# State space tiles: squares added in pairs on GpSimd, their products with ones behind the intra product

## The chip, the cores and the metric

The kernel runs on one core of one Trainium2 chip. The metric is the device time of one launch in microseconds. The kernel before took 3885.12 us (median of 3 runs, 3883.11 to 3887.59).

## The reference

One inference step of a two-layer streaming encoder for a prompt of 1024 frames and 8 samples of 16 frames, 1152 columns in all, width 1024, in float32. The even layer runs RWKV-7 and Mamba-2 as parallel mixers behind one input and one output projection; the odd layer runs HGRN2. Each layer ends in a SwiGLU network. The part that matters here is the Mamba-2 mixer (16 heads of 64, two groups with a state of 128):

```python
cb = jnp.einsum('bclgn,bcsgn->bclsg', cc, bc)
y_intra = jnp.einsum('bclsg,bclsgh,bcsghp->bclghp', cb, decay_ls, xd)
...
y_inter = jnp.einsum('bclgn,bcghpn,bclgh->bclghp', cc, s_in, jnp.exp(acum))
...
y = y + d_skip[:, None] * xs
y = y.reshape(*y.shape[:2], W_B) * jax.nn.silu(z.astype(jnp.float32))
return group_rms_norm(y, norm_w, G_B), conv_new, s_new
```

`group_rms_norm` divides each of the two groups of 512 channels of a frame by the root of its mean square and weighs it by `norm_w`.

## The kernel before

The stage `mamba_tiles` works on nine tiles of 128 columns: eight of the prompt (t = 0 to 7) and one with all samples (t = 8, LAST). Channels lie on the partitions in eight blocks of 128, the columns of the tile beside each other. Each engine has its own order, written out by hand as a loop over t from -1; in one round the tile t is in its middle part, u = t + 1 in its front part and t - 1 in its last part. Semaphores join the engines.

TensorE, one round: `inter(t)` (L3252, the state product), `square_sum(t - 1)` (L3364), `intra(t)` (L3270, sixteen heads), `turn_x(u)` (L3279, the transposes of the next x), `grams(u)`, half of a transpose of a sample's state (L3324), `turn_y(t)` (L3307), `state(t)` (L3314), the other half, and four `segments(u, i)` (L3301).

VectorE, one round: `inter(t)` (L3113, takes the state product out of PSUM), `finish(t - 1)` (L3129, eight instructions that weigh the tile by root and weight, into `g.act`), `intra(t)` (L3122, adds the intra product), `weigh(u)` (L3138, takes the turned x), `mask_CB(u)` (L3147), `skip(t)` (L3165, eight instructions), `scale_state(t)` (L3151) and `add_state(t)` (L3158), `gate(t)` (L3172), `to_end(u)` (L3178), `scores(u)` (L3184, two instructions that multiply the decays of eight heads each by the masked score).

ScalarE, one round: `spread_decays(u, 0)` (L3020, eight instructions), `root(t - 1)` (L3044 and L3047), `spread_decays(u, 1)`, copies and exponentials (L3051, L3033, L3027), and `square(t)` (L3038), which writes the squares of the gated tile t, 128x1024, into `squares(t)`: a part of `g.act` that belongs to a later tile, for the last tile `zt`.

GpSimd sets a small mask and, when the x of the last tile is there, copies four small pieces (L3099). SP loads x and z: the x of tile u + 1 (L2997) and the z of tile u (L2999) go out when the gate of tile u - 1 is done.

The sum over the channels of a group is a product of `ones` with each of its four blocks of squares, accumulated in PSUM. Waits that touch the change: the intra products wait for `att_done` (the scores) and `xd_done`; VectorE's `intra` waits for them; `weigh` waits for `turn_x`; `skip` waits for `out_done` (the finish before); `square_sum(t)` waits for the squares and for the exponentials of the tile after; `segments` and the transposes of the last state wait for `var_ln`, the first half of the root.

Of the kernel before, what the change touches and what calls it, by code (L numbers as in the profile page):

```python
# [18 lines left out]
ALU = mybir.AluOpType  # L19
# [9 lines left out]
NT = T // P  # L29
# [2922 lines left out]
def mamba_tiles(nc, g, A, S, S_samples, decays, shared, xbc, first_x, states_in, ssm_out, following):  # L2952
# [4 lines left out]
    with Phase(nc, "mamba") as ph:  # L2957
# [11 lines left out]
        squares = lambda t: g.act[:, PAIRS:KACT, (t + 1) * P:(t + 2) * P] if t < NT - 1 else zt[:, :, :]  # L2969
# [1 line left out]
        bank = ph.ps("bank", [P, 8, BANK])  # L2971
        (x_in0, x_in1, z_in, mask_set, RL_done, xT, xd_done, CB_mm, CB_done, B_out, seg_mm, seg_out, att_done, xde_done,
         inter_mm, intra_mm, y1_done, y2_done, st_mm, S_scaled, S_done, yT, skip_done, yz_done, sq_done, ss_mm, var_ln,
         rs_done, out_done, Ce_done, xde_split, seq_scaled, seq_T, seq_in, last_T, last_out) = ph.sems(
            "x_in0 x_in1 z_in mask_set RL_done xT xd_done CB_mm CB_done B_out seg_mm seg_out att_done xde_done "
            "inter_mm intra_mm y1_done y2_done st_mm S_scaled S_done yT skip_done yz_done sq_done ss_mm var_ln "
            "rs_done out_done Ce_done xde_split seq_scaled seq_T seq_in last_T last_out")
        stored = ph.sems("out0 out1 out2")
        x_in = (x_in0, x_in1)
        block = ph.block()  # L2980
        LAST = NT - 1
# [29 lines left out]
        @block.scalar  # L3011
        def _(act):
            nc.scalar.preload_act_table_set("natural_log_exp_and_others")

            def spread_decays(u, half):
                if u:
                    act.wait_ge(seg_mm, 4 * u)
                mask = g.notafter if u == LAST else g.notafter128
                for h in range(half * GH, half * GH + GH):
                    ins = nc.scalar.activation(RL[:, h, :], mask[:, :], ACT.Identity, scale=decays.tok[:, 1, u, h:h + 1])  # L3020
                ins.then_inc(RL_done, 1)

            def take_B(u):
                act.wait_ge(CB_done, u + 1)
                if u >= 2:
                    act.wait_ge(st_mm, u - 1)
                nc.scalar.copy(B_tok[:, u % 2, :, :].rearrange("p g n -> p (g n)"), bank[:, 2, 256:512]).then_inc(B_out, 1)  # L3027

            def take_seg(u, i):
                act.wait_ge(seg_mm, 4 * u + i + 1)  # L3030
                if u:
                    act.wait_ge(intra_mm, u)
                nc.scalar.activation(att[:, i * QH:(i + 1) * QH, :].rearrange("p h l -> p (h l)"), bank[:, i % 2, :],  # L3033
                                     ACT.Exp, scale=-1.0).then_inc(seg_out, 1)

            def square(t):
                act.wait_ge(yz_done, t + 1)
                nc.scalar.activation(squares(t), y[:, :, :], ACT.Square).then_inc(sq_done, 1)  # L3038

            def root(t):  # L3040
                act.wait_ge(ss_mm, t + 1)
                if t:
                    act.wait_ge(out_done, t)
                nc.scalar.activation(rs[:, :, :].rearrange("p g c -> p (g c)"), bank[:, sums_at(t), 0:256], ACT.Ln,  # L3044
                                     bias=g.eps[:, 1:2], scale=1.0 / (WB // 2)).then_inc(var_ln, 1)
                act.wait_ge(var_ln, t + 1)
                nc.scalar.activation(rs[:, :, :], rs[:, :, :], ACT.Exp, scale=-0.5).then_inc(rs_done, 1)  # L3047

            def take_sequence(b, i):
                act.wait_ge(seq_T, 2 * b + i + 1)  # L3050
                nc.scalar.copy(S_samples[:, b, i * BANK:(i + 1) * BANK], bank[:, 3, :]).then_inc(seq_in, 1)  # L3051

            def take_rows(i):
                act.wait_ge(last_T, i + 1)
                if i >= 3:
                    act.wait_ge(stored[row_of(i)], 16 * (i // 3))
                for half in range(2):
                    nc.scalar.copy(rows[:, row_of(i), half * BANK:(half + 1) * BANK], bank[:, (6 if i else 0) + half, :]
                                   ).then_inc(last_out, 1)

            for t in range(-1, NT + 1):
                u = t + 1
                if u <= LAST:
                    spread_decays(u, 0)
                if 1 <= t:
                    root(t - 1)
                if t == LAST:
                    take_rows(0)
                if u <= LAST:
                    spread_decays(u, 1)  # L3070
                    if 0 <= t:
                        take_sequence(t, 0)
                    take_seg(u, 0)
                    take_seg(u, 1)
                    take_B(u)
                    if 0 <= t:
                        take_sequence(t, 1)
                    take_seg(u, 2)
                    take_seg(u, 3)
                if 0 <= t <= LAST:  # L3080
                    square(t)
            for i in range(1, SEQS):
                take_rows(i)

        @block.gpsimd
        def _(pool):
            tt = nc.gpsimd.tensor_tensor
            pairs = g.blockmask[:, :].rearrange("p (i e) -> p i e", e=2)
            tt(mask_e[:, :], pairs[:, 0, :], pairs[:, 1, :], ALU.add).then_inc(mask_set, 1)
            for i in range(2, 4):  # L3090
                pool.wait_ge(mask_set, i - 1)
                tt(mask_e[:, :], mask_e[:, :], pairs[:, i, :], ALU.add).then_inc(mask_set, 1)
            nc.gpsimd.memset(C_e[:, :, :, :], 0.0).then_inc(mask_set, 1)
            pool.wait_ge(*x_ready(LAST))
            pool.wait_ge(mask_set, 4)
            v = lambda ap: ap.rearrange("p g (i e c) -> p g i e c", e=2, c=BLK)
            for e in range(2):
                for gr in range(2):
                    ins = nc.gpsimd.tensor_copy(v(C_e[:, :, e, :])[:, gr, :, e, :],  # L3099
                                                v(xbc[:, LAST % 2, KB + 2:NXBC, :])[:, gr, :, e, :])  # L3100
            ins.then_inc(Ce_done, 1)

        @block.vector
        def _(dve):
# [102 lines left out]
            for t in range(-1, NT):  # L3207
                u, mid = t + 1, 0 <= t <= LAST
                if mid:
                    inter(t)  # L3210
                if 1 <= t:
                    finish(t - 1)
                if mid:
                    intra(t)
                    if t == LAST:
                        split_rows()
                        scale_sequence(0)
                if u <= LAST:
                    weigh(u)
                    mask_CB(u)  # L3220
                if mid:
                    skip(t)
                if mid and t < LAST:
                    scale_state(t)
                    add_state(t)
                if mid:
                    gate(t)
                if u <= LAST:
                    to_end(u)
                    scores(u)  # L3230
# [10 lines left out]
        def _(pe):  # L3241
# [112 lines left out]
                ins.then_inc(st_mm, 1)  # L3354

            def square_sum(t):
                pe.wait_ge(sq_done, t + 1)
                if t < LAST:
                    pe.wait_ge(seg_out, 4 * (t + 2))
                else:  # L3360
                    pe.wait_ge(y1_done, NT)
                for i in range(2):
                    for j in range(4):
                        ins = mm(bank[:, sums_at(t), i * P:(i + 1) * P], g.ones[:, :], squares(t)[:, 4 * i + j, :],  # L3364
                                 start=(j == 0), stop=(j == 3))
                ins.then_inc(ss_mm, 1)

            for t in range(-1, NT):
                u, mid, front = t + 1, 0 <= t <= LAST, t + 1 <= LAST
                if mid:  # L3370
                    inter(t)
                if 1 <= t:
                    square_sum(t - 1)
                if mid:
                    intra(t)
                if t == LAST:
                    turn_last(0)
                if front:
                    turn_x(u)
                    grams(u)  # L3380
                    if mid:
                        turn_sequence(t, 0)
                if mid:
                    turn_y(t)
                    if t < LAST:
                        state(t)
                if front:
                    if mid:
                        turn_sequence(t, 1)
                    for i in range(4):  # L3390
                        segments(u, i)
# [681 lines left out]
```

## Time and profile before

| | |
|---|---|
| median of 3 runs | 3885.12 us (3883.11 to 3887.59) |
| profiled execution | 3885.76 us |
| its span, first to last instruction | 3884.0 us |
| TensorE, matmul busy | 3580.7 us (92%) |
| VectorE busy | 2126.4 us (55%) |
| ScalarE busy | 1045.1 us (27%) |
| GpSimd busy | 1424.0 us (37%) |
| mean granted TensorE clock | 0.962 of full speed |

The busy times are of the whole program. The stage of the state space tiles is a small part of it, in the eleventh and twelfth of the page's forty slices. In a timeline row the first number is the start, the second the time to the end of the last instruction of the row; rows of different operations can overlap by up to some 0.15 us, since an instruction starts while the one before it drains. Matrix products in float32 show as two records each.

### The profile page before, as it was taken

The page shows a single profiled execution, that of the slowest core. Times are in us where ns is not written, and L with a number is a line of the kernel's source. Part 1 is how long each engine was busy: PE and PEld are TensorE (multiplying, and loading weights), DVE is VectorE, ACT ScalarE, POOL GpSimd, SP SyncE. Part 2 cuts the span into 40 slices and gives each one's busy share as a digit, 9 for nine tenths or more (in the row PEclk, how much of TensorE's full clock was granted, in tenths as well). Part 3 has the DMA queues.
Part 4 walks back from the last instruction along what each step waited for, and adds up shares of the span by engine and source line. Part 5 has one row for each costly group of instructions (what it writes and reads, how often), then busy time and mean ns, then how long its engine had stood idle before and what let it go on. Part 6 is the DMA issues. An engine that isn't in the chain of part 4 may idle for free. (4 is left out here: it accounts for less than half of the span.)

```text
span 3884.0 us, 69453 instructions
## 1 busy us (share of the span) xinstructions
PE 3580.7 (92%) x29720; PEld 3378.2 (87%) x29720; DVE 2126.4 (55%) x3054; ACT 1045.1 (27%) x1716; POOL 1424.0 (37%) x1147
## 2 busy tenths in 40 slices
PE   7999978887989799999999999978869699999998
PEld 6999967776659799999999999977759699999998
DVE  5543655763884745554545544346665655545545
ACT  2000125552640233333100232024430333333100
POOL 4222222120012377777422322220013577776331
PEclk8999989998999899999999999989979899999999
DMA  6455531103331022222322133232231122222321
GB/s 217 163 173 178 175 97 31 29 15 73 77 97 38 23 62 74 73 70 74 120 90 63 63 111 121 80 101 83 83 115 44 34 69 68 74 74 93 108 89 71
DMA packets 393189, 339.26 MB, mean 87 GB/s; under 512 B 19683, under 2 KB 363233, under 8 KB 386766
## 3 DMA queue, kind: packets, MB, share of 16 engines
q1 hardware_dynamic: 381568, 290.89, 24.6%
q10 hardware_dynamic: 11214, 44.33, 2.8%
q8 instruction: 214, 3.51, 0.4%
q0 software_dynamic: 128, 0.00, 0.2%
q14 instruction: 65, 0.53, 0.0%
HBM read 249.95 MB, written 85.24 MB: 86 GB/s over the span
## 5 line engine op out<-in xcount | busy, mean ns | idle before, releaser
L1295 PE MATMUL ffn_acc<-ffn_BH,ffn_WH 128*128 128x384 f32 x1232 | 417.8, 339 | 40.2 <-DVE ffn_BL L1498 29.3
L1295 PE MATMUL ffn_acc<-ffn_BL,ffn_WH 128*128 128x384 f32 x1232 | 417.0, 338 | 0.0
L1295 PE MATMUL ffn_acc<-ffn_BH,ffn_WL 128*128 128x384 f32 x1232 | 416.6, 338 | 0.0
L1218 POOL TENSOR_TENSOR ffn_WL<-raw,ffn_WH 128x512 fp32r<-128x512 f32 x180 | 284.4, 1582 | 273.1 <-ACT ffn_WH L1384 273.1
L1708 PE MATMUL ffn_acc<-ffn_BH,ffn_WH 128*128 128x384 f32 x1056 | 353.8, 335 | 8.7 <-DVE ffn_tmp L1784 4.5
L1708 PE MATMUL ffn_acc<-ffn_BL,ffn_WH 128*128 128x384 f32 x1056 | 353.3, 335 | 0.0
L641 PE MATMUL in_ab_acc<-hH,in_ab_wH 128*128 128x384 f32 (+2 forms) x840 | 288.6, 344 | 7.0 <-DVE hL L502 6.9
L641 PE MATMUL in_ab_acc<-hL,in_ab_wH 128*128 128x384 f32 (+2 forms) x840 | 285.1, 339 | 0.0
L1218 POOL TENSOR_TENSOR ffn_WL<-ffn_S,ffn_WH 128x512 fp32r<-128x512 f32 x176 | 272.2, 1557 | 30.3 <-ACT ffn_WH L1384 30.3
L1295 PEld LDWEIGHTS ffn_acc<-ffn_BH,ffn_WH 128*128 128x128 f32 x1232 | 234.0, 190 | 44.6 <-issue 32.0
L641 PE MATMUL in_c_acc<-hH,in_c_wH 128*128 128x384 f32 (+1 forms) x768 | 260.8, 340 | 6.8 <-DVE hL L502 6.8
L1295 PE MATMUL ffn_acc<-ffn_hH,ffn_WH 128*128 128x394 f32 x704 | 242.6, 345 | 25.0 <-POOL ffn_hL L1246 17.6
L641 PE MATMUL in_c_acc<-hL,in_c_wH 128*128 128x384 f32 (+1 forms) x768 | 260.6, 339 | 0.0
L1295 PE MATMUL ffn_acc<-ffn_hH,ffn_WL 128*128 128x394 f32 x704 | 242.7, 345 | 0.0
L1295 PE MATMUL ffn_acc<-ffn_hL,ffn_WH 128*128 128x394 f32 x704 | 242.7, 345 | 0.0
L1708 PE MATMUL ffn_acc<-ffn_BH,ffn_WL 128*128 128x384 f32 x1056 | 240.3, 335 | 0.0
L1780 DVE SCALAR_TENSOR_TENSOR xT<-ffn_acc,mod,xT 128x768 f32<-128x768 f32 x96 | 97.6, 1017 | 256.1 <-PE ffn_acc L1708 256.1
L1295 PEld LDWEIGHTS ffn_acc<-ffn_BL,ffn_WH 128*128 128x128 f32 x1232 | 234.4, 190 | 0.3
L1295 PEld LDWEIGHTS ffn_acc<-ffn_BH,ffn_WL 128*128 128x128 f32 x1232 | 234.4, 190 | 0.0
L1708 PEld LDWEIGHTS ffn_acc<-ffn_BH,ffn_WH 128*128 128x128 f32 x1056 | 198.8, 188 | 10.0 <-POOL ffn_WL L1680 5.0
L1708 PEld LDWEIGHTS ffn_acc<-ffn_BL,ffn_WH 128*128 128x128 f32 x1056 | 198.8, 188 | 0.0
L641 PE MATMUL in_ab_acc<-hH,in_ab_wL 128*128 128x384 f32 (+2 forms) x840 | 196.5, 339 | 0.0
(620 smaller groups left out, 8255.3 us busy)
## 6 DMA issues: line engine op xcount, KB each, us to landing
in_ab_ada<-in_ada_w SPq DMA_DIRECT2D x40, 1024.0 KB, 5.0
hidden<-ffn_up SPq DMA_DIRECT2D x44, 576.0 KB, 2.8
raw<-in_w_gate SPq DMA_DIRECT2D x44, 512.0 KB, 3.8
raw<-in_w_up SPq DMA_DIRECT2D x44, 512.0 KB
raw<-in_w_down SPq DMA_DIRECT2D x80, 256.0 KB, 2.7
pT<-in_ab_out ACTq DMA_DIRECT2D x34, 576.0 KB, 3.4
pT<-in_c_out ACTq DMA_DIRECT2D x32, 576.0 KB, 3.7
raw<-in_w_in_ab SPq DMA_DIRECT2D x34, 512.0 KB, 4.8
```

What stands on the lines that cost most here:

```text
L641: ins = self.nc.tensor.matmul(self.acc[0:rows, u, c, 0:n], w[:, u, k, 0:rows], x[:, k, c * CH:c * CH + n], start=(k == 0 and w is self.wH ...
L1218: self.nc.gpsimd.tensor_tensor(self.WL[:, slot], src, self.WH[:, slot].bitcast(F32), ALU.subtract).then_inc(lo, 1)
L1295: ins = self.nc.tensor.matmul(self.acc[:, bank, 0:n], w[:, slot, k, :], x(low, k), start=start and k == 0 and w is self.WH and low == 0, s ...
L1708: ins = nc.tensor.matmul(acc[:, pair + c if c < 2 else third, 0:CH], w[:, slot, k, :], x[:, k, chunk(c)], start=k == 0 and w is m.WH and x ...
L1780: stt(xs, acc[:, pair:pair + 2, 0:CH], gate[:, n, 0:1], xs, ALU.mult, ALU.add)
```

## The change

The squares of a tile are added two by two on GpSimd (block 2 to block 0 and block 3 to block 1 of each group, one instruction of 128x512), for all tiles but the last. `square_sum` then has two products per group in place of four; for the last tile it is as before. On TensorE it moves behind `intra(t)`, on VectorE `finish(t - 1)` moves behind `mask_CB(u)`, on ScalarE `root(t - 1)` behind the second half of `spread_decays`. The addition of tile 7 stands behind the four copies on GpSimd.

```diff
@@ scalar
                 if u <= LAST:
                     spread_decays(u, 0)
+                    spread_decays(u, 1)
                 if 1 <= t:
                     root(t - 1)
                 if t == LAST:
                     take_rows(0)
                 if u <= LAST:
-                    spread_decays(u, 1)
                     if 0 <= t:
                         take_sequence(t, 0)
@@ gpsimd
+            def add_squares(t):
+                v = squares(t).rearrange("p (g n) c -> p g n c", n=4)
+                pool.wait_ge(sq_done, t + 1)
+                tt(v[:, :, 0:2, :], v[:, :, 0:2, :], v[:, :, 2:4, :], ALU.add).then_inc(sq_added, 1)
+            for t in range(LAST - 1):
+                add_squares(t)
             pool.wait_ge(*x_ready(LAST))
...
             ins.then_inc(Ce_done, 1)
+            add_squares(LAST - 1)
@@ vector
                 if mid:
                     inter(t)
-                if 1 <= t:
-                    finish(t - 1)
                 if mid:
                     intra(t)
...
                 if u <= LAST:
                     weigh(u)
                     mask_CB(u)
+                if 1 <= t:
+                    finish(t - 1)
                 if mid:
                     skip(t)
@@ tensor
             def square_sum(t):
-                pe.wait_ge(sq_done, t + 1)
                 if t < LAST:
+                    pe.wait_ge(sq_added, t + 1)
                     pe.wait_ge(seg_out, 4 * (t + 2))
+                    parts = 2
                 else:
+                    pe.wait_ge(sq_done, NT)
                     pe.wait_ge(y1_done, NT)
+                    parts = 4
                 for i in range(2):
-                    for j in range(4):
+                    for j in range(parts):
                         ins = mm(bank[:, sums_at(t), i * P:(i + 1) * P], g.ones[:, :], squares(t)[:, 4 * i + j, :],
-                                 start=(j == 0), stop=(j == 3))
+                                 start=(j == 0), stop=(j == parts - 1))
...
                 if mid:
                     inter(t)
+                    intra(t)
                 if 1 <= t:
                     square_sum(t - 1)
-                if mid:
-                    intra(t)
```

## Rows read from the trace of the kernel before

**Rows 1.** Windows of the stage: length, each engine's busy time, granted clock, DMA.

```profile
1060.00:1076.00 16.00, 16.00 (x97) 11.48 (x96) 15.37 (x30) 10.09 (x28) 0.00 (x0) 1.00 0.34 85
```

**Rows 2.** Timeline of TensorE, first tile: start, length, engine, line, idle before, releaser.

```profile
978.49 3.79 PE L3270 MATMUL mamba_bank<-mixer_shared,raw 128*128 128x64 f32 x32 [0.23 <-DVE raw L3184]
982.11 1.04 PE L3279 MATMUL mamba_bank<-ident,mb_xbc 128*128 128x128 f32 x8
```

**Rows 3.** Timeline of VectorE, first tile.

```profile
977.21 1.23 DVE L3184 TENSOR_TENSOR raw<-raw,mamba_CBm 128x1024 f32<-128x1024 f32 x1 [0.95 <-ACT raw L3033]
982.31 1.28 DVE L3122 TENSOR_TENSOR mamba_y_tok<-mamba_y_tok,mamba_bank 128x512 f32<-128x512 f32 x2 [2.68 <-PE mamba_bank L3270]
```

**Rows 4.** Timeline of TensorE, seventh tile.

```profile
1072.60 1.89 PE L3252 MATMUL mamba_bank<-mb_S,mb_xbc 128*128 128x512 f32 x4
1074.39 2.05 PE L3364 MATMUL mamba_bank<-act,ones 128*128 128x128 f32 x16
1076.28 3.72 PE L3270 MATMUL mamba_bank<-mixer_shared,raw 128*128 128x64 f32 x32
```

**Rows 5.** Timeline of VectorE, seventh tile.

```profile
1077.52 2.19 DVE L3129 SCALAR_TENSOR_TENSOR act<-sumsq,colB,mamba_rs 128x128 f32<-128x128 f32 x8 [0.16 <-ACT mamba_rs L3047]
1080.04 1.28 DVE L3122 TENSOR_TENSOR mamba_y_tok<-mamba_y_tok,mamba_bank 128x512 f32<-128x512 f32 x2 [0.33 <-PE mamba_bank L3270]
1081.24 1.28 DVE L3138 TENSOR_TENSOR mixer_shared<-mamba_bank,mb_tok 128x512 f32<-128x512 f32 x2
1082.44 0.41 DVE L3147 TENSOR_TENSOR mamba_CBm<-mamba_bank,notafter 128x256 f32<-128x256 f32 x1
1082.89 2.16 DVE L3165 SCALAR_TENSOR_TENSOR sumsq<-mb_xbc,dskip,mamba_bank 128x128 f32<-128x128 f32 x8
1084.96 1.22 DVE L3151 TENSOR_TENSOR mb_S<-mb_S,mb_dec 128x1024 f32<-128x1024 f32 x1
1086.29 1.22 DVE L3158 TENSOR_TENSOR mb_S<-mb_S,mamba_bank 128x1024 f32<-128x1024 f32 x1
1087.43 1.22 DVE L3172 TENSOR_TENSOR sumsq<-sumsq,mamba_zt 128x1024 f32<-128x1024 f32 x1
...
1089.70 2.36 DVE L3184 TENSOR_TENSOR raw<-raw,mamba_CBm 128x1024 f32<-128x1024 f32 x2
```

**Rows 6.** Timeline of TensorE, fifth tile, the turn of x.

```profile
1048.00 1.09 PE L3279 MATMUL mamba_bank<-ident,mb_xbc 128*128 128x128 f32 x8 [0.97 <-DMA mb_xbc<-pT]
```

**Rows 7.** Timeline of VectorE, fourth and fifth tile.

```profile
1038.57 1.22 DVE L3172 TENSOR_TENSOR sumsq<-sumsq,mamba_zt 128x1024 f32<-128x1024 f32 x1
...
1049.13 1.29 DVE L3138 TENSOR_TENSOR mixer_shared<-mamba_bank,mb_tok 128x512 f32<-128x512 f32 x2 [0.78 <-PE mamba_bank L3279]
```

**Rows 8.** Timeline of TensorE, intra products of the second and the last tile.

```profile
994.45 3.72 PE L3270 MATMUL mamba_bank<-mixer_shared,raw 128*128 128x64 f32 x32
...
1109.94 3.68 PE L3270 MATMUL mamba_bank<-mixer_shared,raw 128*128 128x64 f32 x32
```

**Rows 9.** Timeline of ScalarE: squares of a tile, second half of a root.

```profile
1105.08 1.05 ACT L3038 ACTIVATE act<-sumsq 128x1024 f32<-128x1024 f32 x1
...
1110.64 0.42 ACT L3047 ACTIVATE mamba_rs<-mamba_rs 128x256 f32<-128x256 f32 x1
```

**Rows 10.** Timeline of GpSimd in the feed-forward stage.

```profile
1322.20 1.50 POOL L1218 TENSOR_TENSOR ffn_WL<-raw,ffn_WH 128x512 fp32r<-128x512 f32 x1 [3.23 <-ACT ffn_WH L1384]
```

**Rows 11.** Timeline of VectorE in the feed-forward stage.

```profile
1321.95 2.16 DVE L1490 SCALAR_TENSOR_TENSOR ffn_BL<-xT,scale,ffn_BH 128x384 fp32r<-128x384 f32 x2
...
1340.88 2.21 DVE L1490 SCALAR_TENSOR_TENSOR ffn_BL<-xT,scale,ffn_BH 128x384 fp32r<-128x384 f32 x4 [2.15 <-ACT ffn_BH L1387]
```

**Rows 12.** Windows: granted clock behind the busy times.

```profile
638.00:640.00 2.00, 0.81 (x2) 0.49 (x3) 1.31 (x5) 1.96 (x4) 0.00 (x0) 1.00 0.00 0
...
1122.00:1124.00 2.00, 2.00 (x9) 2.00 (x10) 2.00 (x2) 0.00 (x0) 0.00 (x0) 0.50 0.00 0
```

**Rows 13.** Timeline of TensorE, sums of the last tile.

```profile
1121.95 3.56 PE L3364 MATMUL mamba_bank<-mamba_zt,ones 128*128 128x128 f32 x16 [1.92 <-ACT mamba_zt L3038]
```

More of the change, by code:

```diff
@@ L2973, in mamba_tiles @@
          inter_mm, intra_mm, y1_done, y2_done, st_mm, S_scaled, S_done, yT, skip_done, yz_done, sq_done, ss_mm, var_ln,
-         rs_done, out_done, Ce_done, xde_split, seq_scaled, seq_T, seq_in, last_T, last_out) = ph.sems(
+         rs_done, out_done, Ce_done, xde_split, seq_scaled, seq_T, seq_in, last_T, last_out, sq_added) = ph.sems(
             "x_in0 x_in1 z_in mask_set RL_done xT xd_done CB_mm CB_done B_out seg_mm seg_out att_done xde_done "
             "inter_mm intra_mm y1_done y2_done st_mm S_scaled S_done yT skip_done yz_done sq_done ss_mm var_ln "
-            "rs_done out_done Ce_done xde_split seq_scaled seq_T seq_in last_T last_out")
+            "rs_done out_done Ce_done xde_split seq_scaled seq_T seq_in last_T last_out sq_added")
         stored = ph.sems("out0 out1 out2")
```

## The prediction

> **What bounds the kernel now.** I read the page's list of slices for the place of the stage, then the timeline of each engine over two of its tiles, then the windows for the clock. The stage with the state space tiles has nine tiles of 128 columns; all that is changed lies there. In the steady tiles TensorE is busy 16.00 of 16 us and VectorE 15.37 [rows 1], so both look like the bound. What matters is which of them the other waits for. One ring goes through both: VectorE's weighing of the scores (L3184) releases TensorE's intra products (L3270), these release VectorE's intra addition (L3122), and everything that VectorE does between that addition and its next L3184 stands in order behind it. The first tile shows the ring without the two things that the change moves: VectorE stands still for 2.68 us before L3122 while the products run [rows 3], and TensorE starts them 0.05 us after L3184 has ended (977.21 + 1.23 against 978.49) [rows 2, 3]. In the later tiles the same pause holds the finish of the tile before (L3129, eight instructions, 2.19 us), and only 0.33 us of idle time is left [rows 5]. On TensorE the sums over the squares (L3364) run 1.89 us from their start to that of the products [rows 4], in the time in which VectorE is still at L3184. So today both the finish and the sums are paid with time that the ring leaves over.
>
> **Change 1, half of the products with ones.** Sixteen matrix records in 1.89 us [rows 4] are eight products; four go, 0.945 us per tile, eight tiles. The removed time lies before the intra products, which will be released by L3184 alone. I count its removal at nothing, because the ring has that time free; the remaining half moves behind the intra products, in front of the turn of the next tile's x (L3279), and there it counts.
>
> **Change 2, the order on VectorE.** Let A be the start of the intra products. The addition L3122 starts at A + 3.82 [rows 2, 3]. Before the change the finish had been done by then; now nothing is left for VectorE there. The turn of x starts at A + 3.62 [rows 2] + 0.945 for the half sums = A + 4.57. A weighing of x that waits for it starts 1.13 us after it (1048.00 to 1049.13) [rows 6, 7], so at A + 5.70, where 3.82 + 1.20 = 5.02 would have been possible: a new wait of 0.68. The mask L3147 follows after 1.20 (A + 6.90), the next place after 0.45 (A + 7.35) [rows 5]. There the finish now stands: 2.19, and since the skip (L3165) waits for the end of the finish just in front of it, 0.11 more, the distance by which L3158 starts behind the end of L3151, on which it waits in the same way [rows 5]. The skip starts at A + 9.65. From its start to the end of L3184 it is 9.17 (1082.89 to 1089.70 + 2.36) [rows 5], which gives A + 18.82, and the next A comes 0.05 later: a period of 18.87 us. Seven such periods lie between the products of the second and of the ninth tile: 132.1 us, where the trace has 1109.94 - 994.45 = 115.5 [rows 8]. That is +16.6. In the ninth tile the finish stands in front of the skip too, on whose gate, squares and sums the rest of the stage waits: +2.3. Together **+18.9 us**. Both ends of this term: if the weighing did not wait, 7 x 0.68 less (+14.1); if a landing of x is late, a few tenths more.
>
> Is anything else late first? The sums are ready, and the root: its second half starts 0.70 us after TensorE has left the sums (1109.94 to 1110.64) and takes 0.42 [rows 8, 9], so a root that ends about A + 5.7 is there before A + 7.35. All sixteen spreads of decays now stand in front of it on ScalarE; they are issued right behind the squares and are over before the sums are. SP's order is not touched: the load of x for the tile after next is issued when the gate L3172 ends. It took 8.21 us to the start of the turn where TensorE waited for it (1038.57 + 1.22 to 1048.00) [rows 6, 7]; the new ring asks for it 3.41 + 0.05 + 4.57 = 8.03 us after the gate [rows 5], so that wait of today (0.97 in that row) is covered now and costs 0.2 at most, in the slowest landing. This is a gain, and it is in the 115.5 that I subtract from.
>
> **Change 3, the additions on GpSimd.** Eight additions of 128x512 f32, both inputs in SBUF. GpSimd is empty in this stage. They start when ScalarE's squares end: 1.05 us [rows 9], about 2.3 us behind the start of the gate, and TensorE asks for them only behind its intra products, 4 us later. Their 1.5 us (a wait included, [rows 10]) are hidden. But they start when VectorE is at L3184, whose two halves read both inputs from SBUF, and the nearest case in the trace had a price: two L1490 on VectorE, which alone take 1.14 (from four in 2.21), took 2.16 when a GpSimd addition began beside the first of them [rows 10, 11]. The second waited, +1.02. L3184 stands in the ring, so each addition costs the ring 1.02: eight times, **+8.2 us**. The ends: nothing, if both halves of L3184 go first and the addition runs beside L3113, which reads one input from PSUM; 1.5 each (+12), if the whole addition stands in front. I take 1.02, the row nearest to it: two instructions of one line back to back, and the addition begins during the first. The Trainium skill, page "SBUF — State Buffer", section "SBUF: two separate sides", says that VectorE with two SBUF inputs and a GpSimd instruction that reads SBUF hold a shared pair of ports exclusively, and whoever starts first keeps it for the whole instruction. By that rule alone the addition would cost up to its own full length where it goes first; the row shows 1.02 for a GpSimd instruction of 1.50, a part of which was its own wait, and in that the trace agrees.
>
> **Change 4, what the longer ring does to TensorE.** Its work falls to about 15 us of a period of 19.9, and the idle time is not spread: it collects in front of the intra products, where TensorE waits for L3184. L3252 waits for L3158; L3184 ends 4.55 us after L3158 (1087.51 to 1092.06) [rows 5], and L3252 fills 1.8 of that (1072.60 to 1074.39) [rows 4]: 2.7 us idle in front of L3270 without change 3, 3.7 with it. The clock in the trace: after 1.92 us of idle (and little work before) the sums of the last tile ran at a granted clock of 0.50, which is 1.2 GHz, and took 3.56 us [rows 12, 13] where the same sixteen take 2.05 [rows 4]; with 0.81 of 2 us busy it stayed at 1.00, 2.4 GHz [rows 12]. The new pause is longer than the one that fell. So I expect falls, in most tiles, with the intra products in the slow stretch. One fall cost 1.51 us on the row; some of it will lie on idle time or on work with slack. I take 1.1 per tile, eight tiles, **+8.8 us**; the ends are 0 and 2 (a slow stretch that covers nearly all of the products).
>
> **The sum.** 18.9 + 8.2 + 8.8 = 35.9. The profiled execution took 3885.76 us (span 3884.0), which gives 3921.7; it is 0.64 above the median of the runs, so I say 3921.
>
> **Rivals.** (a) TensorE is the bound, and the change is faster. For it: busy 16.00 of 16 [rows 1], the intra products start where the sums end, VectorE waits 0.33 for them [rows 4, 5]. Then 0.945 x 8 = 7.6 us go: 3877.5. It decides from the point where L3184 would have ended before the sums did. Against it: in the first tile, without any sums, VectorE waited 2.68 [rows 3], and the finish in that gap is what made TensorE look as the bound. (b) The order counts alone: the halves of L3184 go first and the clock holds: 18.9, so 3904. For it: TensorE still has work on both sides of the pause. (c) Only one of the two extra costs comes: 27 to 28, so 3912. (d) No change, because the finish fits elsewhere: VectorE would need a pause of 2.2 us behind the mask, and L3165 follows L3147 there without one [rows 5].
>
> **Numbers.** Forecast with all three terms 0.50, (c) 0.25, (b) 0.15, more than 2 us per tile from the clock 0.03, (d) 0.04, (a) 0.03. The range from 3900 to 3933 takes in (b), (c) and the upper ends of terms 3 and 4 together but for their extremes. A difference under 0.2% (8 us) can't be told from none here. Slower 0.93, same 0.04, faster 0.03.
>
> **What would show it.** Right: idle time of about 2.6 us before L3122 in every tile; L3129 behind L3147 with no wait for the root; a wait for L3279 before L3138; periods of L3270 of 19 to 21 us; one half of L3184 over 2 us long, beside GpSimd; windows with a clock of 0.50 between L3252 and L3279. Wrong: periods below 17 us, or L3122 without idle time before it, would break term 2; L3184 of 2.36 for the pair breaks term 3; a clock of 1.00 throughout breaks term 4.

## The result, and the profile after

| | before | after |
|---|---|---|
| median of the runs | 3886.36 us (4 runs) | 3941.89 us (4 runs, 3935.07 to 3944.05) |
| profiled execution | 3885.76 us (span 3884.0) | 3942.94 us (span 3941.2) |
| mean granted TensorE clock | 0.962 | 0.954 |

The ratio is 1.0141 [1.0123, 1.0158]: the change makes the kernel 1.4% slower. I had said 3921 and a range of 3900 to 3933. The direction was right and the size was not; the time lies above the range.

The page of the kernel after already says where to look. Columns are engine, busy time, share and number of instructions:

```profile
PE 3607.6 (92%) x29656; PEld 3402.5 (86%) x29656; DVE 2134.8 (54%) x3054; ACT 1047.1 (27%) x1716; POOL 1442.2 (37%) x1155
```

The 64 records less are the 32 products that were taken out, and yet TensorE is busy 26.9 us longer than the 3580.7 of before. Less work that takes longer points to a lower clock. The timeline of TensorE shows it in the second to fourth tile and in the ninth (start, length, engine, line, records, idle before and its releaser; L3270 of before is L3278 now, L3252 is L3260, L3364 is L3375, L3279 is L3287):

```profile
993.32 7.09 PE L3278 MATMUL mamba_bank<-mixer_shared,raw 128*128 128x64 f32 x32 [2.79 <-DVE raw L3192]
...
1012.10 1.95 PE L3260 MATMUL mamba_bank<-mb_S,mb_xbc 128*128 128x512 f32 x4 [0.90 <-DVE mb_S L3166]
1017.62 7.09 PE L3278 MATMUL mamba_bank<-mixer_shared,raw 128*128 128x64 f32 x32 [3.57 <-DVE raw L3192]
1024.50 2.02 PE L3375 MATMUL mamba_bank<-act,ones 128*128 128x128 f32 x8
1026.32 1.26 PE L3287 MATMUL mamba_bank<-ident,mb_xbc 128*128 128x128 f32 x8
...
1041.72 7.09 PE L3278 MATMUL mamba_bank<-mixer_shared,raw 128*128 128x64 f32 x32 [3.57 <-DVE raw L3192]
...
1162.45 6.34 PE L3278 MATMUL mamba_bank<-mixer_shared,raw 128*128 128x64 f32 x32 [2.18 <-DVE raw L3192]
```

The same 32 records that took 3.72 us in [rows 4] take 7.09, and the half sums, 0.95 by half of [rows 4], take 2.02. In front of the products stands the pause that the prediction spoke of, 3.57 us. VectorE in the same tile (L3184 is L3192, L3122 is L3130, L3138 is L3146, L3147 is L3155, L3129 is L3137, L3165 is L3173):

```profile
1014.14 3.43 DVE L3192 TENSOR_TENSOR raw<-raw,mamba_CBm 128x1024 f32<-128x1024 f32 x2
1017.49 1.28 DVE L3121 TENSOR_TENSOR mamba_y_tok<-mamba_bank,mb_dec 128x512 f32<-128x512 f32 x2
1024.75 1.28 DVE L3130 TENSOR_TENSOR mamba_y_tok<-mamba_y_tok,mamba_bank 128x512 f32<-128x512 f32 x2 [5.98 <-PE mamba_bank L3278]
1027.62 1.29 DVE L3146 TENSOR_TENSOR mixer_shared<-mamba_bank,mb_tok 128x512 f32<-128x512 f32 x2 [1.58 <-PE mamba_bank L3287]
1028.82 0.41 DVE L3155 TENSOR_TENSOR mamba_CBm<-mamba_bank,notafter 128x256 f32<-128x256 f32 x1
1029.15 2.18 DVE L3137 SCALAR_TENSOR_TENSOR act<-sumsq,colB,mamba_rs 128x128 f32<-128x128 f32 x8
1031.44 2.15 DVE L3173 SCALAR_TENSOR_TENSOR sumsq<-mb_xbc,dskip,mamba_bank 128x128 f32<-128x128 f32 x8
```

The addition L3130, which waited 0.33 us in [rows 5], waits 5.98. The finish L3137 doesn't wait for its root and stands behind the mask, so its 2.18 us are now in the ring. The pair of scores takes 3.43 instead of 2.36, beside this addition on GpSimd:

```profile
1014.25 2.23 POOL L3098 TENSOR_TENSOR act<-act 128x512 f32<-128x512 f32 x1 [22.07 <-ACT act L3038]
```

Windows of the same tile, and the stage (length, busy time of TensorE, its weight loads, VectorE, ScalarE, GpSimd, then granted clock and DMA):

```profile
1018.00:1020.00 2.00, 2.00 (x11) 2.00 (x11) 0.76 (x2) 0.85 (x3) 0.00 (x0) 0.50 0.60 142
...
1022.00:1024.00 2.00, 2.00 (x11) 2.00 (x11) 0.00 (x0) 0.00 (x0) 0.00 (x0) 0.50 0.00 0
...
1026.00:1028.00 2.00, 2.00 (x17) 2.00 (x17) 0.41 (x2) 0.89 (x2) 0.00 (x0) 0.81 0.00 0
...
1011.00:1170.00 159.00, 131.49 (x588) 99.82 (x588) 107.15 (x183) 63.42 (x159) 16.35 (x11) 0.77 0.21 53
```

TensorE is at 0.50, which is 1.2 GHz, while the intra products run and until the turn of x, although it is busy 2.00 of 2 us in these windows. Over the stage the clock is 0.77, where [rows 1] has 1.00. Each tile from the second to the ninth has one such stretch. Seven of them last 10.2 us and one (in the sixth tile) 13.7, 85.3 together. Before the change no intra product of these tiles ran at the low clock; the only low stretch there was the 3.4 us at the sums of the last tile [rows 12].

Start-to-start periods of the intra products, read from the starts of their rows in each trace. The last column is the number of tiles (of the second to the ninth) whose products were slowed. "+ 3 products" stands for products without use that fill TensorE's pause:

```
                         first    second to ninth (seven periods, us)           slowed
before                   15.96    16.22 15.95 16.65 17.07 15.94 15.89 17.76     0
after                    16.96    24.30 24.10 24.00 23.95 24.84 23.95 23.99     8
e1  order alone          15.89    22.82 19.56 24.46 24.34 22.84 24.45 24.37     6
e2  additions alone      16.96    21.88 16.96 16.96 16.96 16.96 16.96 16.97     1
e3  after, late adds     15.88    21.93 23.57 23.38 23.01 21.94 23.46 23.06     8
e4  after + 3 products   16.96    19.74 19.75 22.80 19.75 19.75 19.74 22.90     2
e5  e1 + 2 products      15.89    19.56 19.57 (six of this size)       22.83    1
e6  e3 + 2 products      15.89    18.67 18.68 18.67 18.67 18.68 21.52 18.67     1
e7  after, sums later    16.96    24.70 24.32 24.12 24.01 23.95 23.06 24.32     8
e8  before, x early      15.96    15.89 (six of this size)             17.79    0
e9  finish alone         15.96    17.97 18.05 18.05 18.42 18.05 18.05 18.05     0
e10 e7 + e3 + 2 products 15.89    18.72 18.73 (five of this size)      19.12    0
```

Seven periods sum to 169.1 us after and 115.5 before. This table carries most of what follows.

The long periods of before need a word. The periods 16.22, 16.65 and 17.07 of before hold waits for x. The 17.76 holds none, and e8, where the waits for x are gone, still has 17.79 there. In this last period it is TensorE that is late: the scores were done at 1107.94, and the sums held the products back until 1109.94 [rows 8]. TensorE, then VectorE, before:

```profile
1104.48 3.64 PE L3260 MATMUL mamba_bank<-mb_S_samples,mamba_C_e 128*32 128x512 f32 x32
1108.05 2.05 PE L3364 MATMUL mamba_bank<-act,ones 128*128 128x128 f32 x16
```

```profile
1105.59 2.35 DVE L3184 TENSOR_TENSOR raw<-raw,mamba_CBm 128x1024 f32<-128x1024 f32 x2
```

So of the 115.5 us some 2.4 are waits for x and 1.9 are TensorE's own work in front of the ninth tile. A longer ring covers both.

### The profile page after: what moved, and what is told of

The parts are those of the page before. It is cut to its first block and busy times, and to the rows that moved or that the text cites. A ratio compares the mean times of both kernels' runs of the same rounds, so it can differ in the third digit from the quotient of the medians.

```text
span 3941.2 us, 69333 instructions
## 1 busy us (share of the span) xinstructions
PE 3607.6 (92%) x29656; PEld 3402.5 (86%) x29656; DVE 2134.8 (54%) x3054; ACT 1047.1 (27%) x1716; POOL 1442.2 (37%) x1155
```

## The experiments

The theory: three costs add up, the longer ring, the shared port and the clock, and only the clock was sized wrongly. Its rivals: the ring itself is longer than I had worked out; or the additions cost more than the second half of L3192. Each time below stands against the kernel before as measured beside it on the same chip.

**e1, the order alone.** The change without the additions: four products with ones per group, behind the intra products. The cut shows the edit to the kernel after.

```diff
-            for t in range(LAST - 1):
-                add_squares(t)
...
-            add_squares(LAST - 1)
...
-                    pe.wait_ge(sq_added, t + 1)
-                    parts = 2
+                    pe.wait_ge(sq_done, t + 1)
+                    parts = 4
```

> The three moves of the change alone: the sums behind the intra products, the finish behind the mask, the root behind both halves of the spreads; eight products of the squares with ones as before, no additions on GpSimd. Theory (the order lengthens the ring, and TensorE's pause then drops its clock for the whole of the intra products): 18.9 for the order plus 0.945 us per tile for the four extra products = about 26 us over before if the clock stays at 1.00, and, if it falls in the 2.7 us pause as it does in the 3.6 us pause of the changed kernel, about 4.5 us more per tile, near 60 us over before; the two halves of L3184 in 2.36 us. Rival (the additions on GpSimd cause most of it): under 15 us over before.

Measured: 3942.72 against 3889.23, ratio 1.0136 [1.0119, 1.0153], 53.5 us for some 60 expected. That is as much as the whole change lost. The order alone makes the pause and with it the fall. Its timeline of TensorE, third and fourth tile:

```profile
1018.58 3.79 PE L3275 MATMUL mamba_bank<-mixer_shared,raw 128*128 128x64 f32 x32 [2.50 <-DVE raw L3189]
...
1038.14 6.77 PE L3275 MATMUL mamba_bank<-mixer_shared,raw 128*128 128x64 f32 x32 [2.49 <-DVE raw L3189]
```

Two pauses of the same length, one without a fall and one with it. The one full period at 2.4 GHz is 19.56, those of the slowed tiles are 22.8 to 24.5. The sums behind slow products are slow too, where sixteen records take 2.05 in [rows 4]:

```profile
1044.71 3.73 PE L3372 MATMUL mamba_bank<-act,ones 128*128 128x128 f32 x16
```

Windows of the two tiles:

```profile
1018.00:1020.00 2.00, 1.42 (x13) 1.42 (x13) 1.73 (x3) 2.00 (x8) 0.00 (x0) 1.00 1.20 303
...
1042.00:1044.00 2.00, 2.00 (x11) 2.00 (x11) 0.00 (x0) 0.00 (x0) 0.00 (x0) 0.50 0.00 0
```

**e2, the additions alone.** The three orders of the kernel before, with GpSimd's additions and the two-part sums in their old place in front of the intra products. The cut shows the edit to the kernel before.

```diff
+                tt(v[:, :, 0:2, :], v[:, :, 0:2, :], v[:, :, 2:4, :], ALU.add).then_inc(sq_added, 1)
...
-                pe.wait_ge(sq_done, t + 1)
+                    pe.wait_ge(sq_added, t + 1)
+                    parts = 2
```

> The additions on GpSimd alone: squares added in pairs, two products per group, all three orders as before. Theory: the two halves of the scores take 3.4 us in place of 2.36, which costs the ring 1.07 us in eight tiles, 8.5 us; the sums now wait for the addition, which itself waits for the port (2.2 us), so TensorE stands still for some 2.2 us in front of them; if that drops the clock, 3 us more per tile, else under 12 us over before in all. Rival (the port costs nothing in the ring, only the order does): within 3 us of before.

Measured: 3894.93 against 3889.23, 1.0017 [1.0007, 1.0027]. In a later tile, VectorE, then GpSimd and TensorE:

```profile
1032.76 3.42 DVE L3192 TENSOR_TENSOR raw<-raw,mamba_CBm 128x1024 f32<-128x1024 f32 x2
...
1037.30 2.19 DVE L3137 SCALAR_TENSOR_TENSOR act<-sumsq,colB,mamba_rs 128x128 f32<-128x128 f32 x8
```

```profile
1033.37 1.72 POOL L3098 TENSOR_TENSOR act<-act 128x512 f32<-128x512 f32 x1 [15.23 <-ACT act L3038]
```

```profile
1035.15 1.16 PE L3375 MATMUL mamba_bank<-act,ones 128*128 128x128 f32 x8 [1.71 <-POOL act L3098]
1036.23 3.79 PE L3278 MATMUL mamba_bank<-mixer_shared,raw 128*128 128x64 f32 x32
```

The pair takes 3.42 and the period 16.96, which is 1.07 more than the 15.89 of a tile that waits for nothing else. Eight times 1.07 is 8.6. Of this, 4.3 come back, since the longer ring covers the late landings of x (2.4) and TensorE's lateness in front of the ninth tile (1.9). One slowed tile, with a period of 21.88, adds 4.9. The trace thus has 9.2 us more in these periods. The times have 5.7 for the 8.5 to 12 expected, with an interval of 2.7 to 10.5 that holds both. TensorE pauses 1.71 to 1.77 us in front of the sums in seven of the eight tiles, and one of the seven was slowed.

**e3, the additions late.** The change as it is, but GpSimd also waits until VectorE has done the scores of the tile:

```diff
                 pool.wait_ge(sq_done, t + 1)
+                pool.wait_ge(att_done, t + 2)
```

> The changed kernel with each addition on GpSimd held until the scores of the tile after it are done, so that it runs beside L3121 of VectorE, which reads one input from PSUM. Theory: the two halves of the scores are back at 2.36, so 8.5 us under the changed kernel for the port; TensorE's pause is 2.7 in place of 3.6 us; if it still drops the clock, about 47 us over before, if it does not, about 19 us over before. Rival (the pair on VectorE and GpSimd is slow for another reason than the shared inputs): as the changed kernel, 55 us over before.

Measured: 3936.15 against 3889.23, 1.0113 [1.0094, 1.0132], 46.9 us for 47 expected, and by the ratios 0.3% below the kernel after, a difference that the two intervals don't separate. The rows show it clearly. VectorE, then GpSimd:

```profile
1013.63 2.35 DVE L3193 TENSOR_TENSOR raw<-raw,mamba_CBm 128x1024 f32<-128x1024 f32 x2
```

```profile
1016.13 1.27 POOL L3099 TENSOR_TENSOR act<-act 128x512 f32<-128x512 f32 x1 [20.66 <-DVE raw L3193]
```

The scores are back at 2.35, and the addition takes 1.27 when it runs beside the inter part of the output (L3122 in this kernel, started at 1015.90), which reads one input from PSUM. So the price of the addition beside the scores is real and can be avoided by place alone. But TensorE's pause is still 2.50 us in six tiles (1.73 in the second, 1.25 in the ninth), and the products of all eight are slow:

```profile
1016.04 7.09 PE L3279 MATMUL mamba_bank<-mixer_shared,raw 128*128 128x64 f32 x32 [2.50 <-DVE raw L3193]
```

**e4, e5, e6, the pause filled.** Useless products with ones, into a bank that is free then, stand in front of the wait for the scores: three per tile on the kernel after (e4), two on e1 (e5), two on e3 (e6). TensorE has more to do in each, and only its idle time is less. The cut is that of e6:

```diff
+            def filler(t):
+                pe.wait_ge(seg_out, 4 * (t + 1))
+                for i in range(2):
+                    mm(bank[:, 1, 0:4 * P], g.ones[:, :], ..., start=True, stop=True)
```

> The changed kernel with three products of 128x512 with ones, whose result nobody reads, in TensorE's pause between the inter and the intra products of tiles 1 to 8 (2.7 us of work in a pause of 3.6). Theory (the clock is what the forecast sized too low): granted clock 1.00 through the stage, intra products in 3.7 us again in place of 7.1, and what is left is order and port, 18.9 + 8.5 = 27 us over before. Rival (the ring is long for another reason and the clock only follows): as the changed kernel or slower, 55 us over before or more.

> The three moves without the additions, with two products of 128x512 with ones in TensorE's pause (1.8 us of a pause of 2.7), whose result nobody reads. Theory (order and clock are two separate terms): the clock stays at 1.00 in most tiles, period of the intra products 18.87 + 0.945 for the four further products = 19.8 us, where e1_order had 19.6 in its one tile without a slow stretch and 22.8 to 24.5 in the others; 26 us over before. Rival (the pause matters for its own sake, not the clock): as e1_order, 53 us over before.

> The changed kernel with the additions held until the scores are done and two products of 128x512 with ones in TensorE's pause. Theory: neither the port nor the clock costs anything, what is left is the order: period 18.87 us, 19 us over before. Rival (part of the order's cost is really the port's or the clock's): under 10 us over before.

Measured: e4 3914.53 against 3889.23, 1.0069 [1.0050, 1.0087], 25.3 us for 27 expected; e5 3907.74 against 3883.30, 1.0052 [1.0035, 1.0068], 24.4 for 26; e6 3907.75, 1.0060 [1.0045, 1.0075], 24.5 for 19. Against their counterparts without the filler (after, e1, e3) the ratios fall by 0.72, 0.84 and 0.53%: added work makes the kernels 28, 33 and 21 us faster. The timeline of TensorE in e4, and its window:

```profile
1010.89 2.74 PE L3275 MATMUL mamba_bank<-level_mask,ones 128*128 128x512 f32 x6
1014.62 3.79 PE L3286 MATMUL mamba_bank<-mixer_shared,raw 128*128 128x64 f32 x32 [0.99 <-DVE raw L3192]
```

```profile
1014.00:1016.00 2.00, 1.38 (x12) 1.38 (x13) 1.77 (x3) 1.85 (x7) 0.00 (x0) 1.00 1.18 282
```

The products are back at 3.79 and the clock at 1.00, in six of eight tiles. This is the run that settles the question: the order and the additions are those of the kernel after, only the three useless products come on top, and a tile takes 4.4 us less. The two tiles of e4 that fell all the same (periods 22.80 and 22.90, products 5.13 and 5.25) are the same instructions in the same execution, some 3.1 us slower. There the fall came only some 2 us after the products had begun (1034.37):

```profile
1034.00:1036.00 2.00, 1.63 (x15) 1.63 (x15) 1.51 (x3) 1.60 (x6) 0.00 (x0) 1.00 1.04 248
1036.00:1038.00 2.00, 2.00 (x14) 2.00 (x14) 0.00 (x0) 0.00 (x0) 0.00 (x0) 0.64 0.00 0
```

The periods give the three terms by subtraction: 18.67 in e6 is the order with the halved sums, 19.74 in e4 is that and the additions beside the scores (+1.07), and 24.16, the mean of the seven after, is that and the clock (+4.4). In e6 the ring can be read without the clock; TensorE, then VectorE (L3131 is L3122 of before, L3147 is L3138):

```profile
1010.16 1.88 PE L3276 MATMUL mamba_bank<-level_mask,ones 128*128 128x512 f32 x4
1012.82 3.79 PE L3287 MATMUL mamba_bank<-mixer_shared,raw 128*128 128x64 f32 x32 [0.78 <-DVE raw L3193]
...
1031.50 3.79 PE L3287 MATMUL mamba_bank<-mixer_shared,raw 128*128 128x64 f32 x32 [0.78 <-DVE raw L3193]
```

```profile
1016.64 1.28 DVE L3131 TENSOR_TENSOR mamba_y_tok<-mamba_y_tok,mamba_bank 128x512 f32<-128x512 f32 x2 [2.68 <-PE mamba_bank L3287]
1018.46 1.29 DVE L3147 TENSOR_TENSOR mixer_shared<-mamba_bank,mb_tok 128x512 f32<-128x512 f32 x2 [0.54 <-PE mamba_bank L3296]
```

The filled kernels are still slower than before, because the ring is still longer. One or two tiles in each were still slowed. In e6 the periods give 7 x 18.67 - 115.5 = 15.2 and the slowed tile 2.85. Behind the last intra products 3.6 us are added: 2.4 until the last tile's sums start, by the order, and 1.2 more, where the clock is low for 10.2 us in place of 3.4. Together some 21.6, and the traced execution of e6 (3906.83) is 21.1 above that of before (3885.76), so the stage holds all of it. The medians lie 24.5 apart.

**e9, the finish alone.** The kernel before, with one line moved on VectorE: the finish behind the mask.

```diff
-                if 1 <= t:
-                    finish(t - 1)
                 if mid:
                     intra(t)
...
                     mask_CB(u)
+                if 1 <= t:
+                    finish(t - 1)
```

> Only the finish on VectorE moves behind the mask; the sums stay in front of the intra products on TensorE, the root between the spreads, no additions. Theory: the finish leaves the ring's pause, which costs 2.3 us per tile less what the waits for x gave back, period 18.2 us, 14 us over before in all; since the sums fill 1.9 us of TensorE's pause, the clock stays at 1.00 in most tiles. Rival (the longer ring alone drops the clock, wherever the sums are): 4 us more per tile, 45 us over before.

Measured: 3896.93 against 3883.30, 1.0035 [1.0023, 1.0047], that is 13.6 us for 14 expected. TensorE keeps the sums in front of the products, so its pause is split into three (1.16, 0.18 and 0.27 us), no tile is slowed, and what is left is the bare ring, 18.05:

```profile
1028.09 2.05 PE L3364 MATMUL mamba_bank<-act,ones 128*128 128x128 f32 x16 [0.18 <-ACT act L3038]
1030.40 3.79 PE L3270 MATMUL mamba_bank<-mixer_shared,raw 128*128 128x64 f32 x32 [0.27 <-DVE raw L3184]
...
1044.00 1.95 PE L3252 MATMUL mamba_bank<-mb_S,mb_xbc 128*128 128x512 f32 x4 [1.16 <-DVE mb_S L3158]
```

```profile
1034.23 1.28 DVE L3122 TENSOR_TENSOR mamba_y_tok<-mamba_y_tok,mamba_bank 128x512 f32<-128x512 f32 x2 [2.68 <-PE mamba_bank L3270]
```

2.68 us of VectorE's time stand empty again, as in [rows 3], while the 2.19 us that had filled them are paid elsewhere: 18.05 - 15.89 = 2.16. TensorE has the same work as before and now waits, so its 16.00 of 16 in [rows 1] was not the bound.

**e7, the half sums later.** The kernel after with the half sums behind the turn of the next x (in the last round they stay), so that VectorE's weighing L3146 would not wait for them.

```diff
-                if 1 <= t:
+                if t == LAST:
                     square_sum(t - 1)
-                if t == LAST:
                     turn_last(0)
                 if front:
                     turn_x(u)
                     grams(u)
+                    if 1 <= t:
+                        square_sum(t - 1)
```

> The changed kernel with the sums moved once more, behind the turn of the next x and the grams (in the last tile they stay where they are). Theory (at the slow clock the half sums take 2.0 us in front of the turn, for which VectorE waits 1.5 to 1.8 us before L3146): the turn starts 2.0 us sooner and that wait goes, but the finish then waits for the root; about 1 us less per tile, some 47 us over before. Rival (the wait for the turn is not in the ring): as the changed kernel, 55 us over before.

Measured: 3943.23 against 3884.97, 1.0147 [1.0130, 1.0164]: 58 us for the 47 expected, a miss. It is no faster than the kernel after. VectorE:

```profile
1050.88 1.29 DVE L3130 TENSOR_TENSOR mamba_y_tok<-mamba_y_tok,mamba_bank 128x512 f32<-128x512 f32 x2 [5.98 <-PE mamba_bank L3278]
1052.58 1.29 DVE L3146 TENSOR_TENSOR mixer_shared<-mamba_bank,mb_tok 128x512 f32<-128x512 f32 x2 [0.42 <-PE mamba_bank L3287]
...
1055.29 0.88 DVE L3137 SCALAR_TENSOR_TENSOR act<-sumsq,colB,mamba_rs 128x128 f32<-128x128 f32 x3 [1.08 <-ACT mamba_rs L3047]
```

The wait for the turn shrinks from 1.58 to 0.42, and the finish now waits 1.08 for its root instead. At the slow clock the chain over the sums and the root is the later of the two.

**e10, all remedies together.** The half sums later, the additions late, and two products in the pause.

> The same with the additions held until the scores are done and two products of 128x512 with ones in TensorE's pause, whose result nobody reads, so that only the order is left. Theory: against e6_late_filler (period 18.67) the wait of 0.68 us for the turn goes and a wait of about 0.5 us for the root comes in front of the finish: period 18.4 to 18.6 us, 18 to 22 us over before. Rival (the two waits do not trade): 18.0 us, as e9_finish, 14 us over before.

Measured: 3906.98 against 3884.97, 1.0053 [1.0037, 1.0070]. 22.0 us for 18 to 22 expected. No tile is slowed, the period is 18.73 where 18.4 to 18.6 was expected. VectorE:

```profile
1035.85 1.28 DVE L3131 TENSOR_TENSOR mamba_y_tok<-mamba_y_tok,mamba_bank 128x512 f32<-128x512 f32 x2 [2.68 <-PE mamba_bank L3287]
1037.05 1.28 DVE L3147 TENSOR_TENSOR mixer_shared<-mamba_bank,mb_tok 128x512 f32<-128x512 f32 x2
...
1039.25 2.19 DVE L3138 SCALAR_TENSOR_TENSOR act<-sumsq,colB,mamba_rs 128x128 f32<-128x128 f32 x8 [0.58 <-ACT mamba_rs L3047]
```

Also at the full clock the wait only changes its name: 0.54 for the turn in e6, 0.58 for the root here.

**e8, x earlier.** The kernel before, with SP issuing the load of x for the tile after next ahead of the wait and the load for z.

```diff
+                        sp.wait_ge(skip_done, u)
+                        sp.wait_ge(inter_mm, u)
+                        sp.dma_start(xbc[:, (u + 1) % 2, :, :], ...)
```

> The kernel before with the load of the next x issued when the skip and the inter product that read the old one are done, ahead of the wait for the gate and of the load of z. Theory: the waits of the turn for x (0.16, 0.60 and 0.97 us in three tiles) go, and with them the waits behind them on VectorE; periods of 15.9 in tiles 2 to 7 where three had 16.3, 16.7 and 17.1; 2.3 us under before, which the times may not tell from none, but the trace does. Rival (the transfer takes as long because z and x then share the queue otherwise, or something else is late next): periods as before.

Measured: 3880.39, 0.9992 [0.9982, 1.0002] against the kernel before. The periods are 15.88 to 15.89 as expected, the waits for x are gone, and TensorE stands busy in all of the stage:

```profile
1003.00:1097.00 94.00, 94.00 (x559) 67.57 (x558) 90.19 (x170) 60.18 (x156) 2.78 (x4) 1.00 0.32 85
```

The sum of the seven periods is 113.1, so 2.4 us less than before; the times give 3 us less and can't be told from no change. It has the lowest median of all, and no proven gain.

## Why the prediction was wrong

By the traces the stretch from the first intra products to the last turn grew by 60.1 us: 53.6 in the seven periods, 1.0 in the first, 5.5 behind the start of the last products. The span grew by 57.2; the other 3 lie outside the stage, within what executions of one kernel differ by.

- **What the ring is: right.** VectorE waits 2.68 us before the intra addition wherever the finish isn't there (e6, e9, e10), and 5.98 where the products are slow. Rivals (a) and (d) are refuted: with the sums out of TensorE's way the periods from the second to the eighth tile grew in every kernel that moved them, and e9 shows the order's cost with TensorE's work unchanged. Only in front of the ninth tile was TensorE the bound, as (a) has it.
- **Change 1, removing half of the sums is worth nothing in their old place: right in the tiles with a steady period, wrong for the ninth.** In e2 the sums are halved, and the period moves by 1.07 alone, the price of the additions. In front of the ninth tile the sums did hold the products back by 1.9 us before. The forecast missed this and yet counted it, because it took seven whole periods from the measured 115.5. That was luck.
- **Change 2, +18.9: right.** I had a period of 18.87 for the order with halved sums and no port; e6 has 18.67. The new wait before the weighing is 0.54 where I had 0.68. Seven periods give 15.2 for 16.6. In the last tile the sums start 14.40 us behind the intra products in e6 and e9 and 12.01 before, so 2.4 for the 2.3 of the forecast. Together 17.6. With the halved sums the waits for x went as said.
- **Change 3, +8.2: right.** 1.07 per pair where I took 1.02 from [rows 10, 11]; seven and the 1.0 of the first period are 8.5. The row of the feed-forward stage was a good stand-in: here too it is two instructions of one line, and GpSimd's addition gets in between them. The Trainium skill, page "SBUF — State Buffer", section "SBUF: two separate sides", says that the two engines hold the shared ports in turns of whole instructions; the traces agree: the addition takes 1.27 us in e3, away from the scores, and 2.23 and 1.72 beside them, and the price to VectorE is nearly the length of the addition in e3, 1.07 of 1.27, and goes to nothing there.
- **Change 4, +8.8: the step that failed.** Its mechanism was right (falls in most tiles, the products in the slow stretch) and its size was wrong: measured 7 x (24.16 - 19.74) = 30.9, and some 3.1 of the 5.5 behind the last products, where slow products and sums stand on the way to the end. That is 34.0 in place of 8.8. The 25 us between them, less the 3 outside the stage and 1 from the other two terms, are the 21 that the forecast lacks. I had taken "one fall cost 1.51 us on the row" for the price of a fall. But [rows 13] holds only about 2 us of work, and the low stretch around it was itself short, 3.4 us by these windows of before (0.93, 0.50 in [rows 12], 0.72):

```profile
1120.00:1122.00 2.00, 0.08 (x2) 0.05 (x1) 2.00 (x3) 1.06 (x1) 0.00 (x0) 0.93 0.00 0
...
1124.00:1126.00 2.00, 2.00 (x15) 2.00 (x14) 2.00 (x3) 0.45 (x1) 0.00 (x0) 0.72 0.04 8
```

After the change a stretch lasts 10.2 us, and the work behind it doubles: the products, 7.09 - 3.79 = 3.3; the half sums, 1.82 to the turn's start in place of 0.95, 0.87; the turn 0.2. All three lie in the ring, one behind the other, so nothing of it is hidden: 4.4 per tile. I also discounted it ("some of it will lie on idle time or on work with slack"), although my own step had just put these three into the ring. The upper bound of 2 was wrong by the same error: the products alone at half the clock, 3.7 us more, were to be read from [rows 4], and my bound "covers nearly all of the products" didn't do that sum. The case of "more than 2 us per tile" had a chance of 0.03. The words "and little work before" were a misreading too, of no weight for the size: up to the pause of 1.92 us TensorE had worked for 3.69 us (L3352, at 1116.33).

As an estimate from these rows, a tile whose clock falls before its products costs 3.7 + 0.95, 37 us over eight tiles. With 18.9 + 8.2 the upper end would have been 3950. The measured time lies inside that.

Rival (b), the order alone, came out as a time only in the filled and split kernels. Unfilled, the order alone cost 53 us (e1), as much as the whole change: what the additions cost beside the scores (1.07) they give back in sums of half the length, which stand in the ring now (3.73 against 2.02, rows of e1 and after). So the periods with nearly all products slow are 24.4 in e1 and 24.0 after.

**Left open.** Why the clock stays at 0.50 for 10 us with TensorE busy nearly throughout, and why one pause of 2.5 us is followed by a fall and the next isn't, no run here tells. Longer or shorter products behind the same pause would be a test; it wasn't made.

## What to carry to other kernels

An instruction that fills an idle gap of a ring over two engines is free only there; moved behind the released work it costs its whole length (2.19 us moved, 2.16 us per period), whatever the busy shares say. Where a change opens a pause on TensorE as long as one that ended in a fall in your rows, price the fall at the doubled length of what follows in the ring, as here, and not at what one fall cost on a short row elsewhere. A useless product in the pause is a cheap test of that: if more work makes the kernel faster, look at the clock.

## What the runs showed of the hardware

- Pause in front of the intra products, and the tiles whose products were then slowed: 3.57 us (after, e7), 6 of 6 in each, and 2.79 and 2.18 (after), 2.80 and 2.93 (e7), all four; 2.50 (e3), 6 of 6, and 1.73 and 1.25, both; 2.50 (e1), 5 of 6, and 1.73, but not 1.77; 1.71 to 1.77 in front of the sums (e2), 1 of 7; 0.99 (e4), 2 of 6; 0.78, 1 of 6 in e5 and in e6 and none of 6 in e10. Except for e2 these kernels pause some 0.9 us more per tile in front of the state product. e9, with 1.16, 0.18 and 0.27, has none slowed. More idle time, more falls, but the length of one pause does not decide it.
- The fall can come after the pause: in e4 TensorE had been busy for some 2 us again before the clock went from 1.00 to 0.50.
- Once at 0.50 the clock stayed there for 10.2 us in seven tiles of the kernel after and for 13.7 in one, while TensorE was busy 2.00 of 2 us in most windows, on 128x64 products in float32. In the slowed tiles of e4, e5 and e6 it stayed for 6.8 us.
- One 128x512 addition in float32 on GpSimd takes 1.27 us beside a VectorE instruction that reads one input from PSUM, and 1.72 or 2.23 beside the scores, both of whose inputs are in SBUF; it came in between the two instructions in all eight tiles of the kernel after, and the pair grew from 2.36 to 3.43.
